# An MoE decoder step on one core: gated sums inside a written-out last round, the last tile as 128 half rows, h one tile a round

## The reference, cut to what matters

```python
h = layer_norm(DEEPNORM_ALPHA * x + gate1 * (merged @ w_o), ln1_g, ln1_b)
v = h * (1 + scale2) + shift2
f = moe_ffn(v.reshape(Bn * T, D), w_router, b_router, w_up, b_up, w_down, b_down)
y = layer_norm(DEEPNORM_ALPHA * h + gate2 * f.reshape(Bn, T, D), ln2_g, ln2_b)
```

## Time and profile before

| what | us |
|---|---|
| median of 3 runs | 1294.69 (1293.08 to 1295.81) |
| the profiled execution | 1289.3, of it 1287.5 from its first to its last instruction (the span) |
| TensorE busy | 1198.5 |
| VectorE busy | 563.7 |
| ScalarE busy | 255.8 |
| GpSimd busy | 160.7 |

### The profile page before, as it was taken

How to read it: one execution, slowest core, us unless ns; L and a number is a source line. 1 busy time by engine, 2 the same in 40 slices (tenths; PEclk the granted TensorE clock), 3 DMA queues, 4 the chain that set the end, 5 groups by cost and what they waited for, 6 DMA issues and landing times.

```text
span 1287.5 us, 17057 instructions
## 1 busy us (share of the span) xinstructions
PE 1198.5 (93%) x5960; PEld 517.8 (40%) x5961; DVE 563.7 (44%) x1059; ACT 255.8 (20%) x404; POOL 160.7 (12%) x96
## 2 busy tenths in 40 slices
PE   5999999979999999899999999999999999999991
PEld 2688885523333333333333333333333333333330
DVE  0507815774443443344433444433444434434457
ACT  1523210242112111111112111212111211111121
POOL 0556462045200000000000000000000000000024
PEclk9999999989999999999999999999999999999995
DMA  9966696469999999999987999997999999699961
GB/s 334 349 248 263 247 301 227 145 257 419 406 427 427 427 426 426 425 426 426 428 379 300 427 425 428 426 428 303 377 427 427 428 426 426 262 424 426 427 252 41
DMA packets 54780, 466.33 MB, mean 362 GB/s; under 512 B 5511, under 2 KB 5671, under 8 KB 18633
## 3 DMA queue, kind: packets, MB, share of 16 engines
q1 hardware_dynamic: 52809, 460.11, 87.0%
q0 software_dynamic: 1952, 5.97, 1.4%
HBM read 464.29 MB, written 1.77 MB: 362 GB/s over the span
## 4 chain that ended last, share of the span: by engine, by line
PE 63%; DMA 26%; DVE 8%; ACT 1%; POOL 1%; issue 1%; SPq 0%; DVEq 0%; ACTq 0%; POOLq 0%
PE bank L909 26%; DMA ring<-in_w_up 24%; PE bank L943 12%; PE bank L695 8%; PE bank L885 3%; PE bank L746 3%; PE bank L763 2%; DMA ring<-in_w_ada 2%; PE bank L810 2%; PE bank L637 1%; PE bank L681 1%; PE bank L934 1%; DVE front L1407 1%; POOL front L547 1%; ACT front L1100 1%
## 5 line engine op out<-in xcount | busy, mean ns | idle before, releaser
L909 PE MATMUL bank<-ring,front 128*64 128x512 f32 x2240 | 504.7, 596 | 21.0 <-DMA ring<-in_w_up 21.0
L909 PEld LDWEIGHTS bank<-ring,front 128*64 128x64 f32 x2240 | 152.8, 137 | 314.4 <-issue 268.8
L943 PE MATMUL bank<-ring,front 128*64 128x512 f32 x1120 | 250.7, 601 | 6.8 <-ACT front L1100 6.8
L1380 DVE TENSOR_TENSOR front<-front,bank 128x512 f32<-128x512 f32 (+1 forms) x210 | 143.9, 685 | 56.8 <-PE bank L885 35.1
L1366 DVE TENSOR_TENSOR O_parts<-bank,O_parts 64x512 fp32r<-64x512 f32 x70 | 48.2, 689 | 239.2 <-ACT O_parts L1066 234.7
L943 PEld LDWEIGHTS bank<-ring,front 128*64 128x64 f32 x1120 | 77.9, 138 | 155.8 <-issue 142.0
L1097 ACT ACTIVATE front<-front 128x256 f32<-128x256 f32 x70 | 29.2, 417 | 504.3 <-DVE front L1398 504.3
L579 POOL TENSOR_TENSOR parts_home<-front 128x1024 f32<-128x1024 f32 (+1 forms) x2 | 5.2, 2576 | 917.8 <-DVE onehot_T L1421 917.8
L1398 DVE TENSOR_SCALAR front<-bank 128x256 f32<-128x256 f32 x70 | 29.7, 425 | 163.7 <-PE bank L909 162.5
L885 PE MATMUL bank<-O_parts,onehot_T 128*128 128x512 f32 x216 | 81.3, 454 | 11.2 <-DVE front L1446 6.5
L1066 ACT ACTIVATE O_parts<-bank 64x512 fp32r<-64x512 f32 x70 | 41.4, 591 | 237.5 <-PE bank L943 236.7
(11 more groups left out here) (217 smaller groups left out, 871.5 us busy)
## 6 DMA issues: line engine op xcount, KB each, us to landing
ring<-in_w_up SPq DMA_DIRECT2D x128, 2048.0 KB, 18.2
ring<-in_w_down SPq DMA_DIRECT2D x128, 1024.0 KB, 17.5
ring<-in_w_ada SPq DMA_DIRECT2D x12, 2048.0 KB, 11.9
ring<-in_w_in SPq DMA_DIRECT2D x7, 2048.0 KB, 8.0
ring<-in_w_o SPq DMA_DIRECT2D x2, 2048.0 KB, 21.0
hx<-in_x_prompt SPq DMA_DIRECT2D x2, 1024.0 KB, 8.2
ring<-in_w_in SPq DMA_DIRECT2D x4, 512.0 KB, 22.3
ring<-in_w_out_a SPq DMA_DIRECT2D x1, 2048.0 KB, 7.6
```

Of the source, the lines that this page charges most:

```text
L909: last = mm(bank[B_UP[j]][64 * h:64 * h + 64, :], x_T[:, (c % 2) * 2 + b, 64 * (c // 2):64 * (c // 2) + 64], w[:, :, at:at + 256], start=F ...
L943: last = mm(bank[B_DOWN][64 * h:64 * h + 64, :], act_T[:, 2 * j + b, 64 * hh:64 * hh + 64], expert_chunk_at(UP_CHUNKS + m)[:, b * 1024 + h ...
L1380: signal(TT(Y[0:r, 2 * t + h, :], Y[0:r, 2 * t + h, :], bank[b][0:r, :], ALU.add), bank_free[b], value)
```

## The change

1. VectorE's loop ends one round earlier (`final` = G - 1), and the last round is written out. In it, after `add_up` of each tile, VectorE multiplies `Y` by gate2 and adds h, in place (`gate_and_add_h`). For tile 2 this puts the right half of each row on partitions 64 to 127, so that 64 rows of 1024 become 128 half rows of 512. GpSimd's products for tiles 1 and 2 go.
2. In the tail the next tile's product of bank and gate2 is made inside `normalise`, ahead of the reciprocal. The last `combine` of tile 2 writes the two halves of each row into the two halves of one bank, with plain FP32 operands; tile 2 is normalised on 128 partitions, with copies between the upper and the lower 64, and stored by two transfers.
3. Tile i of h waits for the cast of round i + 1.
4. GpSimd loads the right half of the samples' gate2 for partitions 64 to 127, and both halves of ln2_g and ln2_b for the half rows: 12 more loads.

```diff
--- before
+++ after
+        norm2_pairs = region(front, 4 * D, 2, 512)
+        share = region(front, 8292, 2, 512)
...
                 pool.wait_ge(row_normed, i + 1)
+                pool.wait_ge(onehot_ready, i + 3)
                 pool.tensor_tensor(row, row, norm1_rows[0:r, 0, :], ALU.mult).then_inc(h_step, 1)
...
+                pool.dma_start(tail_rows[NS_TOK + TSEQ * s:NS_TOK + TSEQ * (s + 1), D:D + 512],
+                               mod_rows[1 + s, 5 * D + 512:].partition_broadcast(TSEQ)).then_inc(tail_landed, 16)
...
-            pool.wait_ge(onehot_ready, G + 1)
-            pool.wait_ge(bank_full[B_X], G + front_uses(B_X) + 1)
-            for i, t in enumerate((1, 2)):
-                r = ROWS[t]
-                gate2 = tail_rows[0:r, (t // 2) * D:(t // 2 + 1) * D]
-                pool.tensor_tensor(out_rows[0:r, t, :], Y[0:r, 2 * t:2 * t + 2, :].rearrange("p h d -> p (h d)"), gate2,
-                                   ALU.mult).then_inc(gated_ready, 1)
-                pool.wait_ge(gated_ready, i + 1)
-                pool.tensor_tensor(out_rows[0:r, t, :], out_rows[0:r, t, :], hx[0:r, t, :], ALU.add).then_inc(sum_ready, 1)
-
+            for i, name in enumerate(("ln2_g", "ln2_b")):
+                for h in range(2):
+                    pool.dma_start(norm2_pairs[NS_TOK * h:NS_TOK * (h + 1), i, :],
+                                   a[name][0, h * 512:(h + 1) * 512].partition_broadcast(NS_TOK)).then_inc(tail_landed, 16)
...
-            pool.dma_start(outs[2], out_rows[0:NS_TOK, 2, :]).then_inc(out_stored, 16)
+            for h in range(2):
+                pool.dma_start(y_s[:, h * 512:(h + 1) * 512], out_rows[NS_TOK * h:NS_TOK * (h + 1), 2, 0:512]).then_inc(out_stored, 16)
...
-            for t in range(3):
+            for t in range(2):
                 combine(G, t)
+            pe.wait_ge(bank_free[B_C[0]], front_uses(B_C[0]) + PER_ROUND[B_C[0]] * G + 2)
+            for h in range(2):
+                last = mm(bank[B_C[0]][NS_TOK * h:NS_TOK * (h + 1), :], onehot_T[:, 2 * P:NT].bitcast(F32),
+                          O_parts[:, h, :].bitcast(F32), start=True, stop=True)
+            last.then_inc(bank_full[B_C[0]], 1)
...
+            def gate_and_add_h(t):
+
+                r = ROWS[t]
+                rows = Y[0:r, 2 * t:2 * t + 2, :].rearrange("p h d -> p (h d)")
+                sum_up(TT(rows, rows, gate2(t), ALU.mult))
+                if t < 2:
+                    sum_up(TT(rows, rows, hx[0:r, t, :], ALU.add))
+                else:
+                    for h in (1, 0):
+                        sum_up(TT(Y[r * h:r * h + r, 4, :], Y[0:r, 4 + h, :],
+                                  hx[0:r, 2, h * 512:(h + 1) * 512], ALU.add))
...
             round_work(0)
-            with dve.Fori(1, G) as g:
+            with dve.Fori(1, final) as g:
                 low_of_result(g, bank[B_DOWN])
                 round_work(g)
+            low_of_result(final, bank[B_DOWN])
+            dve.wait_ge(tail_landed, 16 * (7 + 2 * NSEQ))
+            dve.wait_ge(h_ready, 3)
+            round_work(final, after_sum=gate_and_add_h)
...
+            for t in range(2):
                 for h in range(2):
...
+                    if h or not t:
+                        gated(t, h)
+                    half = out_rows[:, t, h * 512:(h + 1) * 512]
+                    step(TT(half, Y[:, 2 * t + h, :], share[:, h, :], ALU.add))
+                    step(v.bn_stats(stats[:, 6 * h:6 * h + 6], half))
+                normalise(P, meanwhile=lambda: gated(t + 1, 0))
+
+            pair = out_rows[:, 2, 0:512]
+            lower, upper = slice(0, NS_TOK), slice(NS_TOK, P)
+            step(TT(pair, Y[:, 4, :], share[:, 0, :], ALU.add))
+            step(v.bn_stats(stats[:, 0:6], pair))
+            step(v.tensor_copy(stats[lower, 6:12], stats[upper, 0:6]))
+            step(v.bn_aggr(aggr[lower, :], stats[lower, :]))
...
+            step(v.tensor_copy(aggr[upper, 0:1], aggr[lower, 0:1]))
+            step(STT(pair, pair, aggr[:, 0:1], norm2_pairs[:, 0, :], ALU.subtract, ALU.mult))
...
+            step(v.tensor_copy(rstd[upper, :], rstd[lower, :]))
+            signal(STT(pair, pair, rstd, norm2_pairs[:, 1, :], ALU.mult, ALU.add), y_ready, 1)
```

More of the change, by code:

```diff
@@ L315, in program @@
         y_ready = sem("y_ready")
-        gated_ready = sem("gated_ready")
-        sum_ready = sem("sum_ready")
+        sum_step = sem("sum_step")
         block = ctx.enter_context(nc.Block())
@@ L567, in _ @@
                                mod_rows[1 + s, 5 * D:].partition_broadcast(TSEQ)).then_inc(tail_landed, 16)
+                pool.dma_start(tail_rows[NS_TOK + TSEQ * s:NS_TOK + TSEQ * (s + 1), D:D + 512],
+                               mod_rows[1 + s, 5 * D + 512:].partition_broadcast(TSEQ)).then_inc(tail_landed, 16)
             pool.dma_start(tail_rows[:, 2 * D:3 * D], a["ln2_g"][0].partition_broadcast(P)).then_inc(tail_landed, 16)
             pool.dma_start(tail_rows[:, 3 * D:], a["ln2_b"][0].partition_broadcast(P)).then_inc(tail_landed, 16)
-            pool.wait_ge(table_ready, 1)
-            G = pool.value_load(table[0:1, 159:160], min_val=1, max_val=52)
-            pool.wait_ge(tail_landed, 16 * (3 + NSEQ))
-            pool.wait_ge(onehot_ready, G + 1)
-            pool.wait_ge(bank_full[B_X], G + front_uses(B_X) + 1)
-            for i, t in enumerate((1, 2)):
-                r = ROWS[t]
-                gate2 = tail_rows[0:r, (t // 2) * D:(t // 2 + 1) * D]
-                pool.tensor_tensor(out_rows[0:r, t, :], Y[0:r, 2 * t:2 * t + 2, :].rearrange("p h d -> p (h d)"), gate2,
-                                   ALU.mult).then_inc(gated_ready, 1)
-                pool.wait_ge(gated_ready, i + 1)
-                pool.tensor_tensor(out_rows[0:r, t, :], out_rows[0:r, t, :], hx[0:r, t, :], ALU.add).then_inc(sum_ready, 1)
-            outs = (o["y_p"][0, 0:P], o["y_p"][0, P:2 * P], o["y_s"].rearrange("s t d -> (s t) d"))
+            for i, name in enumerate(("ln2_g", "ln2_b")):
+                for h in range(2):
+                    pool.dma_start(norm2_pairs[NS_TOK * h:NS_TOK * (h + 1), i, :],
+                                   a[name][0, h * 512:(h + 1) * 512].partition_broadcast(NS_TOK)).then_inc(tail_landed, 16)
+            outs = (o["y_p"][0, 0:P], o["y_p"][0, P:2 * P])
+            y_s = o["y_s"].rearrange("s t d -> (s t) d")
             for t in range(2):
@@ L1338, in _ @@
             step(TS(table[0:1, NROUND:2 * NROUND], base_f[0:1, :], float(SLOTS), None, ALU.mult))
+            step(TS(table[0:1, 2 * NROUND + E:2 * NROUND + E + 1], ps[0:1, 2 * NROUND + E - 1:2 * NROUND + E], -1.0, None, ALU.add))
             free("table", v.tensor_copy(table[0:1, 2 * NROUND:2 * NROUND + E], ps[0:1, 2 * NROUND:2 * NROUND + E]))
@@ L1370, in _ @@
             dve.wait_ge(cleared, 2)
-            G = dve.value_load(table[0:1, 159:160], min_val=1, max_val=52)
+            G = dve.value_load(table[0:1, 159:160], min_val=E, max_val=52)
+            final = dve.value_load(table[0:1, 160:161], min_val=E - 1, max_val=51)
             def add_up(n, t):
@@ L1383, in _, with sum_up, round_work @@
             PER_LOOP = 4
-            def round_work(g):
+            sums = [0]
+            def sum_up(ins):
+                sums[0] += 1
+                signal(ins, sum_step, sums[0])
+            gate2 = lambda t: tail_rows[0:ROWS[t], (t // 2) * D:(t // 2 + 1) * D]
+            def gate_and_add_h(t):
[8 more added lines that the diff above has]
+                                  hx[0:r, 2, h * 512:(h + 1) * 512], ALU.add))
+            def round_work(g, after_sum=lambda t: None):
                 steps[0] = 0
@@ L1409, in round_work @@
                 add_up(g, 0)
+                after_sum(0)
                 dve.wait_ge(bank_full[B_T], g * 2 + front_uses(B_T) + 1)
@@ L1414, in round_work @@
                 add_up(g, 1)
+                after_sum(1)
                 clamp(0)
@@ L1428, in _ @@
             steps[0], origin[0], step_sem[0] = 0, 0, tail_step
-            dve.wait_ge(tail_landed, 16 * (3 + NSEQ))
-            dve.wait_ge(h_ready, 3)
             dve.wait_ge(bank_full[B_X], G + front_uses(B_X) + 1)
[L1433 to L1436, removed]
@@ L1437, in _ @@
             low_of_result(G, bank[B_DOWN])
[L1438 to L1441, removed]
-                for h in range(2):
[L1443 to L1452, removed]
@@ L1454, in _, with gated @@
-            r, row = ROWS[2], out_rows[0:ROWS[2], 2, :]
-            normalise(r, meanwhile=lambda: step(STT(row, row, aggr[0:r, 0:1], tail_rows[0:r, 2 * D:3 * D], ALU.subtract, ALU.mult)))
-            signal(STT(row, row, rstd[0:r, :], tail_rows[0:r, 3 * D:], ALU.mult, ALU.add), y_ready, 1)
+            def gated(t, h):
+                b = B_C[h]
+                value = G * PER_ROUND[b] + (front_uses(b) + t + 1)
+                dve.wait_ge(bank_full[b], value)
+                gates = gate2(t)[:, h * 512:(h + 1) * 512] if t < 2 else tail_rows[:, D:D + 512]
```

(16 more changed lines are left out.)

3 lines of the change are left out of this document (2 added, 1 removed).

## The result

The changed kernel takes 1298.61 us (median of 7 runs, 1297.65 to 1301.02), the kernel before 1293.08 on the same chip (7 runs): a ratio of 1.0043, 95% interval 1.0034 to 1.0053. It is slower by 5.5 us. The forecast was no change, 1294.4, and a range that ended at 1296.6.

What follows compares the result with a forecast made beforehand. Up to about 664 us the loaded bytes bound the kernel, at its end a VectorE, ScalarE and GpSimd chain. Terms +2.0 - 2.1 - 0.2 = -0.3 us gave 1294.4 us against the median 1294.69, range 1290.6 to 1296.6.

Steps and rivals of the forecast that it cites:

- New loads, +2.0 us: GpSimd's 12 extra loads, 0.66 MB, near 390 us in the saturated stretch: +2.0 us, bounds 1.5 and 3.8.
- the loads cost by the piece: Rival: near 390 us the new loads cost 3.8 us instead of 2.0, giving 1296.2 us; chance 0.16.
- h, one tile a round, 0: Round 1 loses 3.65 us of VectorE waiting for GpSimd's h, but DMA is saturated there: gain costed at nothing.
- Round 1 is on the path: Rival: shortening round 1 gains its whole 3.65 us, giving 1290.7 us; chance 0.15.
- the loads are hidden: Rival: holes in the saturated stretch near 390 us absorb the new loads' 2.0 us, giving 1292.4 us; chance 0.15.
- The written-out last round, +0.3: VectorE's added operations in the last round make the clamp and down product about 0.3 us late, bounds 0 and 1.
- the start of the tail, -2.1 with it: Tile 0's work is done earlier, so T0, the first bank-and-gate product, comes 2.1 us earlier, the 0.3 included.
- From T0 to the last store, -0.2: From the tail's first bank-and-gate product to the end of the last store's issue: 23.85 us instead of 24.07.
- The copy is free: Rival: tile 2's copy of six statistics does not wait for GpSimd, giving 1293.7 us; chance 0.2.
- Sum: All terms together, +2.0 - 2.1 - 0.2 = -0.3 us: 1294.4 us on the median's scale, no change.

Runs made afterwards that it cites:

- with copies: The changed kernel with five on-chip GpSimd copies in place of the 12 new loads: 1291.18 us, 0.9984 of the kernel before.
- the three wide loads: The changed kernel with the same 0.66 MB in 3 loads with two-dimensional repetition instead of 12: 1300.98 us, 1.0063 of the kernel before.

## Why the prediction was wrong

*New loads, +2.0 us*, is the step that failed. It priced 0.66 MB "by the bytes of that queue", with 3.8 us, "a 2 KB piece costing as much as one of 4 KB", as the upper end. The loads cost 6.3 us of stretch when added alone to the kernel before, 6.8 in the changed kernel (7.4 less the 0.6 that stay with copies). The row behind it, 1.55 MB in 25.3%, counts the time of that queue's own packets. The damage is in the packets beside them (for 0.52 MB on 64 partitions against 128, 3.0 us in the expert queue and 0.4 in its own), so the share of that queue could not show it. The rival "the loads cost by the piece" had the sign and the place near 390 us, but not the cause: pieces of 2 KB on all partitions cost their bytes. The trace of before had a hint that I did not read: its windows were taken over 50 and 100 us, and one of 10 us behind the old loads is low (kernel before):

```profile
330.00:340.00 10.00, 10.00 (x50) 3.26 (x46) 1.38 (x2) 2.46 (x3) 0.00 (x0) 1.00 1.00 357
```

There eight of the eleven old loads cover 8 partitions each.

The Trainium skill, SBUF — State Buffer, section "Door 1: The DMA port swizzle (why `[64,N]` ≈ `[32,N]`)", has the rule that would have warned: a transfer's rate goes with how many of the 16 ports its partitions reach, eight for 32 or 64 partitions, two for partitions 64 to 71. An estimate by that page, from the bytes at this case's 427 GB/s, is 2 x 1.2 us for the four loads and 8 x 0.3 for the eight, 4.8 us in all. The runs agree that 64 partitions are no better than 32 (both +4.8 us). The eight loads come near their estimate (2.2 us), the four to twice theirs (4.6); why is open, and so the agreement on the eight may be chance. What lies inside the DMA engines no run shows.

*h, one tile a round, 0*: the mechanism was right. Round 1 got 3.7 us shorter and the stretch no shorter; the hold even costs 0.6 us in the stretch, 0.14% by its ratio, for a reason that no run shows. *Round 1 is on the path* falls with it, and *the loads are hidden* fell at once.

*The written-out last round, +0.3, and the start of the tail, -2.1 with it*: right in kind, 1.8 us gained; the 0.3 that is missing is the round's 0.7 in place of 0.3.

*From T0 to the last store, -0.2*: right, -0.3. The copy waits, as chosen between its bounds: 2.23 us for six numbers. *The copy is free* falls.

*Sum*: with 6.8 for the loads and 0.6 for the hold in place of 2.0, and -1.8 and -0.3 for the rest, the terms make +5.3 us. Measured: 5.5.

## What to carry to other kernels

Beside a saturated stream, price a small load by how many partitions one transfer covers and by what it does to the stream, not by its bytes or its own queue's time. Load all 128 partitions at once, with the 128 rows as the pattern's outermost dimension (the three wide loads, with outer steps of 2 and 8, were the dearest form tried), and copy on chip; or issue it where the DMA engines are idle: the profile's windows, in pieces of 10 us, show both the damage and the gaps. Where the share stays at 1 and GB/s falls, look for what holds the transfers up, not for more bytes.

## What the hardware showed that I had not expected

The same 0.52 MB cost 1.0 to 1.3 us on 128 partitions and 4.8 us on 64 or 32. A load of 128 KB landed in 2.8 us on nearly idle engines and in 30 to 34 us beside the stream. A VectorE copy of 64x6 took 2.23 us, to the end of a GpSimd operation; one of 64x1 took 0.15 us inside GpSimd's next operation.
